# Reordered attention, query projection and tail, and a hot stage with two plain and two gated one-hots per engine, in a mixer and PEER block on one core

## The reference, cut to what matters

```python
(shift1, scale1, gate1, shift2, scale2, gate2) = silu(c) @ W_ada + b_ada
h = rms_norm(x) * (1 + scale1) + shift1
# one input projection of h: pooling channels, q latent, kv latent, rope key
# A: causal pooling over windows 2, 4, 8, 16 minus itself, a linear map per group
# B: 8 heads of attention with a chunk mask:
sc = (einsum('bqhd,bkhd->bhqk', q_nope, k_nope) + einsum('bqhr,bkr->bhqk', q_pe, k_pe)) * scale
p = softmax(where(mask, sc, NEG_INF)); o = einsum('bhqk,bkhd->bqhd', p, v)
y = concat(A, B) @ w_out;              x = x + gate1 * rms_norm(y)
h = rms_norm(x) * (1 + scale2) + shift2
q = (h @ w_q).reshape(t, 8, 2, 128)
sc = einsum('thpd,hpnd->thpn', q, sub_keys)     # 128 keys, two halves
# top 16 of each half, top 16 of their 256 sums -> 128 experts a token, softmax gates
a = einsum('ted,td->te', take(expert_u, idx), h)
out = einsum('te,ted->td', gelu(a) * gate, take(expert_v, idx));   x = x + gate2 * rms_norm(out)
```

## Time and profile before

| | |
|---|---|
| median of 3 runs | 2120.65 us |
| the profiled execution, its own time | 2118.86 us |
| its span, first to last instruction | 2116.9 us |
| mean granted TensorE clock | 0.964 |
| busy: PE, DVE, ACT, POOL | 90%, 71%, 44%, 33% |
| DMA | 439 MB, 207 GB/s over the span |

### The profile page before, as it was taken

The page is one execution under the profiler, slowest core; times in us unless marked ns, Lnnn a source line. Parts: engine busy times, 40 slices in busy tenths (PEclk is TensorE's granted clock), DMA queues, the critical chain, the costliest instruction groups (busy, mean ns, idle before and its releaser), DMA issues.

```text
span 2116.9 us, 34290 instructions
## 1 busy us (share of the span) xinstructions
PE 1914.9 (90%) x10307; PEld 1631.0 (77%) x10307; DVE 1503.8 (71%) x2182; ACT 936.1 (44%) x1438; POOL 689.1 (33%) x414
## 2 busy tenths in 40 slices
PE   0489889799899999999999996689999999999995
PEld 0479658699788888888888885578887888788884
DVE  6898479743688889998886759967775554455554
ACT  1153233453544444445544446644444444444442
POOL 1000020000688888889974448810000000000001
PEclk9799859899999999999999999999999999999997
DMA  9989469992576666666677761057766666665553
GB/s 391 414 315 369 156 253 365 269 227 42 130 189 185 184 186 187 185 184 174 185 190 192 186 172 61 0 168 291 289 234 188 200 210 200 223 214 192 197 189 109
DMA packets 228754, 439.09 MB, mean 207 GB/s; under 512 B 23442, under 2 KB 158048, under 8 KB 214880
## 3 DMA queue, kind: packets, MB, share of 16 engines
q1 hardware_dynamic: 224496, 414.21, 62.2%
q0 software_dynamic: 4176, 24.23, 3.3%
q10 hardware_dynamic: 32, 0.01, 0.0%
HBM read 434.12 MB, written 4.21 MB: 207 GB/s over the span
## 4 chain that ended last, share of the span: by engine, by line
PE 77%; DVE 9%; issue 4%; ACT 3%; DMA 2%; POOL 2%; DVEq 1%; SPq 1%; ACTq 0%; POOLq 0%
PE ps L880 19%; PE ps L936 11%; PE ps L937 11%; PE ps L939 11%; PE ps L882 10%; PE ps L650 4%; PE ps L652 4%; PE ps L651 4%; DVE acc L1300 3%; DVE hotB L1715 3%; POOL eL L530 2%; PE ps L645 2%; DMA raw<-in_peer_v_dram 1%; DMA i<-consts_dram 1%; DVEq L1715 1%
## 5 line engine op out<-in xcount | busy, mean ns | idle before, releaser
L880 PE MATMUL ps<-h,eH 128*128 128x512 f32 x2048 | 720.3, 397 | 6.7 <-POOL eL L530 6.3
L530 POOL TENSOR_TENSOR eL<-raw,eH 128x1024 fp32r<-128x1024 f32 x224 | 551.7, 2470 | 294.4 <-ACT eH L1160 292.6
L882 PE MATMUL ps<-h,eL 128*128 128x256 f32 x2048 | 573.9, 280 | 0.0
L1746 DVE TENSOR_TENSOR eL<-raw,eH 128x1024 fp32r<-128x1024 f32 x256 | 313.4, 1225 | 300.4 <-ACT eH L1247 300.3
L880 PEld LDWEIGHTS ps<-h,eH 128*128 128x128 f32 x2048 | 384.3, 188 | 101.4 <-POOL eL L530 8.6
L1247 ACT CAST eH<-raw 128x1024 fp32r<-128x1024 f32 x256 | 269.8, 1054 | 391.5 <-PE ps L939 338.6
L1160 ACT CAST eH<-raw 128x1024 fp32r<-128x1024 f32 x256 | 269.2, 1052 | 365.9 <-PE ps L882 291.4
L936 PE MATMUL ps<-eH,aH 128*128 128x512 f32 x1024 | 400.2, 391 | 7.2 <-DVE eL L1746 7.2
L937 PE MATMUL ps<-eL,aH 128*128 128x512 f32 x1024 | 399.7, 390 | 0.0
L1669 DVE STREAM_TRANSPOSE raw<-raw 128x1024 f32<-128x1024 f32 x256 | 317.1, 1242 | 105.5 <-DMA raw<-in_peer_u_dram 98.8
L882 PEld LDWEIGHTS ps<-h,eL 128*128 128x128 f32 x2048 | 386.7, 189 | 0.0
(11 more groups left out here) (265 smaller groups left out, 2430.2 us busy)
## 6 DMA issues: line engine op xcount, KB each, us to landing
raw<-in_peer_u_dram SPq DMA_DIRECT2D x1024, 128.0 KB, 2.9
raw<-in_peer_v_dram SPq DMA_DIRECT2D x256, 512.0 KB, 4.1
ring<-in_ada_w_dram SPq DMA_DIRECT2D x40, 2048.0 KB, 17.3
ring<-in_w_out_dram SPq DMA_DIRECT2D x8, 2048.0 KB, 13.6
ring<-in_peer_wq_dram SPq DMA_DIRECT2D x32, 512.0 KB, 17.7
piece<-in_ada_w_dram POOLq DMA_DIRECT2D x13, 1024.0 KB, 5.7
ring<-in_w_in_dram SPq DMA_DIRECT2D x6, 2048.0 KB, 14.6
ring<-in_w_uq_dram SPq DMA_DIRECT2D x2, 1536.0 KB, 8.9
```

Of the source, the lines that this page charges most:

```text
L530: pool.tensor_tensor(by_k(eL[:, j % RING, :]), turned(raw[:, j % RAW, :]), by_k(eH[:, j % RING, :].bitcast(F32)), ALU.subtract).then_inc(u ...
L880: pe.matmul(ps[:, bank, :], eH[:, slot, k * P:(k + 1) * P], h2[:, kk].rearrange("p a t -> p (a t)"), start=kk == 0, stop=False, skip_group ...
L882: mm = pe.matmul(ps[:, bank, 0:T], eL[:, slot, k * P:(k + 1) * P], h2H[:, kk, :], start=False, stop=kk == KT - 1, skip_group_check=True)
L1746: dve.tensor_tensor(eL[:, slot, :], raw[:, slot, :], eH[:, slot, :].bitcast(F32), ALU.subtract).then_inc(v_lo, 1)
```

## The change

**Attention.** `ada_columns(2)` goes from before k to after the values. The first two pooled groups come first, then the rope transposes, the third group, the scores of heads 0 to 2, and only then the last group, the values, `ada_columns(2)` and the loop over heads. `gate_rows(0)` goes behind the loop. DVE leaves the column of gates and six `ada` steps that stood before the first `maxima` and does them inside the head loop (4, 4, then 2 each, 3 in the last two); ACT copies in the matching order.

```diff
+X1_BANK = (2, 3, 0, 1, 4, 5, 6, 7)
+Q_BANK = (2, 0, 4, 2)
...
+            for tt in range(TT):
+                for q in range(4):
+                    cols = slice(q * W, (q + 1) * W)
+                    sp.wait_ge(out_ready[tt], q + 1)
+                    sp.dma_start(out[0, tt * P:(tt + 1) * P, cols], result[:, tt, cols]).then_inc(out_stored, 16)
+            sp.wait_ge(out_stored, 16 * 4 * TT)
...
+            def turn_keys():
+                ring_arrived(pe, ("keys", 0, 0))
+                keys = ring[where[("keys", 0, 0)][0]][:, 0:2048].rearrange("p (k n) -> p k n", k=KT)
+                for i in range(KT):
+                    if i >= 8:
+                        pe.wait_ge(key_out, i // 4 - 1)
+                    mm = pe.transpose(ps[:, 6 + (i // 4) % 2, (i % 4) * P:(i % 4 + 1) * P], keys[:, i, :], ident)
...
             for n in range(4):
-                if n == 1:
-                    pe.wait_ge(h2_out, KT)
...
+                    if n == 3 and k == 0:
+                        pe.wait_ge(qT_out, 4)
...
+                        mm = split3(ps[:, Q_BANK[n] + j // 2, (j % 2) * T:(j % 2 + 1) * T], wh[:, cols], wl[:, cols],
...
-                    pe.wait_ge(gated, g - 1)
+            def scatter(g, q, gates):
+                if gates is not None:
+                    pe.wait_ge(gated, gates)
                 pe.wait_ge(hot_ready, g + 1)
+                pe.wait_ge(hot_act, g + 1)
                 pe.wait_ge(hot_pool, g + 1)
-                pe.wait_ge(hot_act, g + 1)
                 for t in range(4):
-                    hot = hotA[:, half, t, :] if t < 2 else hotP[:, q, t - 2, :]
-                    mm = pe.matmul(ps[:, half, t * P:(t + 1) * P], hot, hotB[:, half, t, :],
+                    hot = hotA[:, q, t, :] if t < 2 else hotP[:, q, t - 2, :]
+                    mm = pe.matmul(ps[:, 4 + q, t * P:(t + 1) * P], hot, hotB[:, q % 2, t, :],
                                    start=True, stop=True, skip_group_check=True)
                 mm.then_inc(hot_mm, 1)
...
+            for tt in range(TT):
+                pe.wait_ge(v_lo, 2 * (TILES - 2) + 2)
+                v_part(0, 1, tt, False, False)
+                pe.wait_ge(act_lo, TILES)
+                for h in range(2):
+                    pe.wait_ge(v_lo, 2 * (TILES - 1) + (h + 1))
+                    mm = v_part(1, h, tt, False, True)
+                mm.then_inc(tail_mm, 1)
...
             y_squares(3)
+            act.wait_ge(y_rc, 1)
+            act.activation(stat[:, 38:40], stat[:, 36:38], ACT.Sqrt).then_inc(y_rs, 1)
             for j in range(2):
                 weight_high("wq", 0, j)
-            act.wait_ge(y_rc, 1)
-            act.activation(stat[:, 38:40], stat[:, 36:38], ACT.Sqrt).then_inc(y_rs, 1)
...
+                act.activation(h2H[:, k, :], ps[:, X1_BANK[k // 2], (k % 2) * T:(k % 2 + 1) * T], ACT.Identity,
+                               bias=mod2[:, 1, k:k + 1], scale=mod2[:, 0, k:k + 1]).then_inc(h2H_out, 1)
+                if k in (3, 7, 11):
+                    weight_high("wq", 0, 2 + k // 4)
...
+            def hot_first(g, q, first):
                 if not first:
-                    act.wait_ge(hot_mm, g - 1)
+                    act.wait_ge(hot_mm, g - 3)
                 for t in range(2):
-                    last_ = act.activation(hotA[:, half, t, :], iota, ACT.Abs,
+                    last_ = act.activation(hotA[:, q, t, :], iota, ACT.Abs,
...
-                o = hotA[:, half, 0:2, :]
-                act.activation(o, o, ACT.Relu, bias=ones[:, 0:1], scale=-1.0).then_inc(hot_act, 1)
-
...
+                for t in range(2):
+                    last_ = act.activation(hotA[:, q, t, :], hotA[:, q, t, :], ACT.Relu,
+                                           bias=slotT[:, 2, bass.ds(g * 4 + t, 1)],
+                                           scale=minus_gate[:, bass.ds(g * 4 + t, 1)])
+                last_.then_inc(hot_act, 1)
...
-            act.activation(stat[:, 50:52], stat[:, 48:50], ACT.Sqrt).then_inc(y2_rs, 1)
+                act.wait_ge(tail_mm, tt + 1)
+                act.activation(raw[:, 0:2, :].rearrange("p a b -> p (a b)"),
+                               ps[:, 4 * tt:4 * tt + 4, :].rearrange("p a b -> p (a b)"), ACT.Square,
+                               accum_out=stat[:, 46 + tt:47 + tt]).then_inc(y2_sq, 1)
+                act.wait_ge(y2_rc, tt + 1)
+                act.activation(stat[:, 50 + tt:51 + tt], stat[:, 48 + tt:49 + tt], ACT.Sqrt).then_inc(y2_rs, 1)
...
-            gate_column(0, 2, 0, V_B2, V_PO1)
-            ada(6)
...
-            dve.wait_ge(pool_mm, 8)
             for h in range(HEADS + 2):
+                if h == 2:
+                    dve.wait_ge(pool_mm, 8)
...
+                if h == 4:
+                    gate_column(0, 2, 1, V_B2, V_PO1)
                 if h <= HEADS:
-                    ada(2)
+                    ada(4 if h < 2 else 3 if h > 6 else 2)
...
+            weight_low("wq", 0, 0)
...
-            for j in range(2):
-                weight_low("wq", 0, j)
+            weight_low("wq", 0, 1)
...
+                dve.wait_ge(h2H_out, 2 * j + 2)
+                for k in (2 * j, 2 * j + 1):
+                    dve.tensor_scalar(h2T[:, k, :], ps[:, X1_BANK[j], (k % 2) * T:(k % 2 + 1) * T], mod2[:, 0, k:k + 1],
+                                      mod2[:, 1, k:k + 1], ALU.mult, ALU.add).then_inc(h2_out, 1)
+                dve.wait_ge(h2_out, 2 * j + 2)
+                both = slice(2 * j, 2 * j + 2)
...
-                for t in range(4):
+                dve.tensor_tensor(hotB[:, q % 2, 0:2, :], iota.unsqueeze(1).broadcast_to([P, 2, P]),
+                                  slotT[:, 0, bass.ds(g * 4, 2)].unsqueeze(2).broadcast_to([P, 2, P]), ALU.is_equal)
+                for t in range(2, 4):
                     i1, gt = (slotT[:, m, bass.ds(g * 4 + t, 1)] for m in (0, 2))
-                    last_ = dve.tensor_scalar(hotB[:, half, t, :], iota, i1, gt, ALU.is_equal, ALU.mult)
+                    last_ = dve.tensor_scalar(hotB[:, q % 2, t, :], iota, i1, gt, ALU.is_equal, ALU.mult)
...
+            def apply_gates(g, pair):
+                dve.wait_ge(hot_mm, g + 2)
+                a = acts[:, :, bass.ds(g * 4, 8)]
+                w = ps[:, 4 + 2 * pair:6 + 2 * pair, :].rearrange("p b (t i) -> p i (b t)", t=4)
+                dve.tensor_tensor(a, a, w, ALU.mult).then_inc(gated, 1)
...
+            with dve.Fori(1, T // 16) as r:
+                hots(r * 4, 0, False)
+                hots(r * 4 + 1, 1, False)
+                apply_gates(r * 4 - 2, 1)
+                hots(r * 4 + 2, 2, False)
+                hots(r * 4 + 3, 3, False)
+                apply_gates(r * 4, 0)
...
             for tt in range(TT):
-                seq(dve.scalar_tensor_tensor(scaled[:, tt, :], ps[:, 4 * tt:4 * tt + 4, :].rearrange("p a b -> p (a b)"),
-                                             stat[:, 50 + tt:51 + tt], gate2[:], ALU.mult, ALU.mult))
-                dve.nop().then_inc(scaled_ready, 1)
-            add_x1(dve, 1)
+                dve.wait_ge(y2_sq, tt + 1)
+                inverse_mean(stat[:, 48 + tt:49 + tt], stat[:, 46 + tt:47 + tt], D)
+                dve.nop().then_inc(y2_rc, 1)
+                dve.wait_ge(y2_rs, tt + 1)
+                for q in range(5):
+                    if q < 4:
+                        cols = slice(q * W, (q + 1) * W)
+                        dve.scalar_tensor_tensor(scaled[:, tt, cols], ps[:, 4 * tt + q, :], stat[:, 50 + tt:51 + tt],
+                                                 gate2[:, cols], ALU.mult, ALU.mult).then_inc(scaled_ready, 1)
+                    if q:
+                        dve.wait_ge(scaled_ready, 4 * tt + q)
+                        add_x1(dve, tt, q - 1)
```

More of the change, by code:

```diff
@@ L594, in _ @@
                 pool.dma_start(extra[:], v.broadcast_to([P, D])).then_inc(extra_in, 16)
[L595 to L601, removed]
         @block.tensor
@@ L720, in _, with pooled @@
             ring_arrived(pe, ("pool", 0, 0))
[L721 to L735, removed]
+            def pooled(g):
+                pe.wait_ge(z_ready, g + 1)
+                pe.wait_ge(kn_out, 2 * g + 2)
+                for j in range(2 * g, 2 * g + 2):
+                    mm_group(ps[:, KV_BANK[g], (j % 2) * T:(j % 2 + 1) * T],
+                             lambda k: wpl[:, g, k, (j % 2) * P:(j % 2 + 1) * P],
+                             lambda k: zT[:, 2 * g + k, :], 2).then_inc(pool_mm, 1)
+            pooled(0)
+            pooled(1)
             pe.wait_ge(k_roped, 1)
             pe.wait_ge(q_roped, 1)
-            pe.wait_ge(grow_out, 1)
             for tt in range(TT):
@@ L745, in _ @@
             mm.then_inc(qpeT_mm, 1)
+            pooled(2)
             pe.wait_ge(qpeT_out, 1)
@@ L787, in _ @@
                 scores(h)
+            pooled(3)
+            for tt in range(TT):
+                for hh in range(2):
+                    m = tt * 2 + hh
+                    pe.wait_ge(pool_out, 2 * m + 2)
```

(11 more changed lines are left out.)

190 lines of the change are left out of this document (89 added, 101 removed).

## The result

The changed kernel takes 2093.69 us, the median of 4 runs (2083.89 to 2097.45), against 2121.48 for the kernel before, timed beside it: a ratio of 0.9862, 95% interval 0.9824 to 0.9901. Timed again with the experiments it took 2088.59 (6 runs), a ratio of 0.9853 (0.9825 to 0.9881). The forecast of 2094 and its range hold. That the sum came so close is luck: errors of its terms cancelled, as the stages show. Each column is one profiled execution, in us; the last is the changed kernel when it was timed again. A row "to" is a length, the others are times from the start of the span.

What follows compares the result with a forecast made beforehand. PE was taken to bound most of the kernel, DVE the hot stage. Terms -9.5 - 5 - 6 - 6.2 = -26.7 from the median 2120.65 gave 2094 us, own range 2085 to 2103, overall 2076 to 2111.

Steps and rivals of the forecast that it cites:

- What bounds it: Whole kernel: PE bounds U and V, DVE ends last in the hot stage; PE has 77% of the chain.
- Attention, -9.5: Attention: first `turn_probs` moves from 265.00 to near 253.9, the head loop takes 47.9, output projection starts at 301.8; -9.5 us.
- Rivals C and D: Head loop keeps 2.4 GHz, 2086 in all, 10%; output projection waits for its weights, 5 lost, 2099, 8%.
- Second norm and query projection, -5: Second norm and query projection: idle 2.42 and its slow stretch go, fewer copy waits, keys before block 3 cost; -5 us.
- The dip that I gave half a chance to: Query projection, behind the gap for the keys before block 3: a slow stretch costing 1.7, at half a chance.
- Hot stage, -6: Hot stage: a round of four groups takes 6.7 on DVE, 0.36 less than before, over 15 rounds; -6 us.
- the 5.7: Hot stage: DVE's time for four groups without collisions with POOL, before 1.0 is added for delayed compares.
- Rival B: Hot loop runs almost free of collisions, near 5.9 for four groups, 12 us more gained, 2082; 15%.
- Rival E: Hot stage: compare and POOL take the port in turn, a round takes 9.2, stage 32 more, 2132; 6%.
- Tail, -6.2: After the last matmul (T): DVE done at T + 9.85, output lands at T + 13.3 against T + 19.5; -6.2 us.
- the 4.3 behind the last traffic: Tail: the time from the output's landing to the end of the span, 4.3 before, was forecast to stay.
- U and V, 0: U and V: PE is the bound and the change leaves their loops alone, so zero gain.

## Why the prediction was right, by its steps

**What bounds it** held: PE in U and V, DVE in the hot stage and in front of the tail.

**Attention, -9.5: -5.5 in the first profile, -8.2 in the second.** The order worked as forecast, with scores at 237.3 for 236.4. DVE was ready at 253.8 for 253.6. PE's count was short: three scores took 6.25 (237.30 to 243.55), not half of 10.5, and `ada_columns` ran partly at the slow level (the clock fell at 254.8). The loop took 49.1, then 48.4, for 47.9. In the ten profiles of all runs that have this order the output projection starts at 302.4 to 305.7, 5.5 to 8.8 earlier than before, and the loop takes 47.4 to 49.1, so its sum held, and the first profile is the worst of them. Of the first profile's shortfall 1.1 is older: PE came to its first product for q at 203.4 for 202.2, behind one more slow stretch at 118. Rivals C and D did not come: the clock is 0.53 from 251 to 306, and the output projection took 96.6 for 96.1.

**Second norm and query projection, -5: -5.2**, the output projection's 0.5 more included (key scores -10.8, of which 5.5 from before; in the second profile -13.4 and -8.2). The stall of 2.42 went, with its slow stretch, and blocks 1 and 2 wait no more. The dip that I gave half a chance to behind the keys didn't come.

**Hot stage, -6: -1.5** (from U's last matmul to V's first, 119.7 to 118.2). This is the step that failed. I added 1.0 a round for compares that meet POOL, and nothing for hots that do, though the earlier trace rows have such a hot at 0.75 and I had counted it in the round before. The timeline has both: four compares 0.2 longer each (0.8) and two pairs of hots 0.32 longer each (0.6), 1.4 in place of 1.0. That brings the 5.7 back to 7.1, where the kernel before was. Taking POOL's work away gives 6.48 with ACT last, so I had ACT too short as well: below 6.2 forecast, 4 × 1.63 = 6.5 measured, as each group waits 0.17 for its own Abs. Rival B's 5.9 was far off. Rival E's price (9.2) did not come: the pair of hots that started at 1301.74, inside a POOL TENSOR_SCALAR, took no more than the undisturbed 0.51. The Trainium skill (SBUF — State Buffer, "Who interferes with whom") is borne out for the instruction with two SBUF inputs, by 606 ns that become 418 with one input in PSUM. Its exclusive lock for a whole instruction isn't what the records show: the compare of 1299.81 started 0.06 behind a POOL TENSOR_SCALAR of 0.85 and was through at 1300.42, 0.18 before that ended. All 46 compares of the steady loop are through 0.17 to 0.18 before the end of the POOL TENSOR_SCALAR in flight, whether they started 0.04 or 0.14 behind it. So they seem to wait for a fixed point in it; as the profile's spans of POOL are rough, a shorter lock isn't ruled out.

**Tail, -6.2: -11.7.** Up to DVE's last result it was as forecast, T + 9.6 for T + 9.85. Then two terms were off: 256 KB landed in 2.1, not 3.5, and the 4.3 behind the last traffic, which I let stay, was for the most part POOL's DRAIN (3.7) and is gone from the end now that SP issues (5.2 more where POOL issues again).

**U and V, 0: -2.5 and -1.8.** The change leaves their loops alone, so I don't put this down to it. V had a slow stretch at 1822 before and none after, and U's part is told below. So of the 28.3 less in the first profile some 24 are the change's (26.6 in the second). The 4.0 missing in attention and the 4.5 in the hot stage were made good by 5.5 in the tail, which I had too small, and by the 4.3 of U and V: the total is right by luck, the stages in part.

## What to carry to other kernels

Before an operation with two SBUF inputs is put beside a busy GpSimd, count how often GpSimd works, and give every DVE instruction of the loop its share of the wait, not the new one alone. A constant operand in a free PSUM bank can take the clash away, at a price for each read (0.07 us a gated hot here), so look at single instructions and not at their mean. Where an output DMA ends a kernel, look for the stretch between the last traffic and the end of the span, and at which engine's closing it belongs to. And compare by stage: a total that agrees can hide a stage that gained nothing.

## What the runs showed that I had not expected

U runs at one of two paces in each of its two loops, and which one it is differs between profiles. By stretch, PE's busy time and its matmuls, from the middle of the first loop and of the second, before and then after:

```profile
600.00:700.00 100.00, 100.00 (x569) 86.77 (x568) 85.21 (x183) 48.09 (x72) 84.59 (x37) 1.00 0.67 187
1150.00:1240.00 90.00, 90.00 (x521) 79.34 (x521) 62.98 (x66) 44.15 (x66) 38.51 (x16) 1.00 0.75 190
```

```profile
600.00:700.00 100.00, 100.00 (x578) 88.17 (x578) 85.00 (x188) 48.40 (x73) 86.83 (x37) 1.00 0.69 189
1150.00:1240.00 90.00, 90.00 (x511) 78.00 (x511) 62.43 (x64) 42.54 (x63) 38.27 (x16) 1.00 0.73 186
```

PE is busy throughout at a clock of 1.00, and does 569 or 578 matmuls in 100 us. 128 matmuls take 22.19 or 22.61, constant through a loop. The kernel before had the slow pace first and the fast one second, the changed kernel the other way round. Over twelve profiles U took 719.6 to 719.8, 723.8, 726.3 to 727.2 or 730.6 to 730.9, the four combinations, also between runs whose U is the same code. That is 11 us, and would make most of the spread of the times. Both profiles of the changed kernel show the same pair, though, so it isn't shown that one kernel changes its pace from execution to execution; where a build puts its code may set it, too. In the two first loops shown above, the slow pace has 0.233, 0.241 and 0.236 in turn from the start of a matmul of 512 columns to the next matmul, where the fast one has 0.230 each time. What sets the pace stays open.
